# Attention core of a two-layer trunk: values as the stationary operand, probabilities scaled before they are turned

## The reference, cut to what matters

```python
# sparse heads: 8 heads in 2 groups (g) of 4 (r), head width 64, keys and values shared in a group
p_c = masked_softmax(einsum('bqgrd,bngd->bgrqn', qg, k_cmp) * scale, ...)   # 15 compressed blocks
o_c = einsum('bgrqn,bngd->bqgrd', p_c, v_cmp)
o_s = softmax over the keys of the selected blocks, times their values      # branch 0
o_w = softmax over the keys of the window, times their values               # branch 1
o_a = gates[..., 0:1] * o_c + gates[..., 1:2] * o_s + gates[..., 2:3] * o_w
# forgetting heads: 8 heads with keys and values of their own               # branch 2
s_f = einsum('bqhd,bkhd->bhqk', q, kb) * scale + cq[..., None] - cum_t[:, :, None, :]
o_b = einsum('bhqk,bkhd->bqhd', masked_softmax(s_f, causal), vb)
return concatenate([o_a, o_b], axis=-1) @ w_out
```

## Time and profile before

| | |
|---|---|
| median of three runs | 1229.42 us |
| span of the profiled execution | 1227.6 us |
| TensorE busy | 1213.1 us, 99% of the span |
| VectorE busy | 977.8 us, 80% |
| ScalarE busy | 815.7 us, 66% |
| GpSimd busy | 35.5 us, 3% |
| attention core, from its first scores to the output projection | 84.7 to 128.1 us |

### The profile page before, as it was taken

One profiled execution on the slowest core, in us unless ns is written; L12 is line 12 of the kernel. 1 busy time (PEld: TensorE's weight loads), 2 busy tenths in 40 slices (PEclk: granted clock), 3 DMA queues, 4 the chain that ended last, 5 costly groups with the idle time before them and its releaser, 6 DMA issues.

```text
span 1227.6 us, 16109 instructions
## 1 busy us (share of the span) xinstructions
PE 1213.1 (99%) x5992; PEld 1009.8 (82%) x5992; DVE 977.8 (80%) x959; ACT 815.7 (66%) x877; POOL 35.5 (3%) x41
## 2 busy tenths in 40 slices
PE   8999999999999999999999999999999999999997
PEld 6878888888898888888888888888888888888886
DVE  6998564554557478999989989889889889889896
ACT  7765354344375467777777777777777777777773
POOL 0000000000000001100000000000000000000300
PEclk9999999999999999999999999999999999999999
DMA  9730254455534256999999999999999999999992
GB/s 352 306 137 2 102 192 170 170 188 206 206 138 141 101 192 236 392 397 369 413 367 370 407 370 375 408 365 373 407 368 376 399 372 374 392 364 376 399 421 85
DMA packets 53000, 361.42 MB, mean 294 GB/s; under 512 B 6048, under 2 KB 6560, under 8 KB 10944
## 3 DMA queue, kind: packets, MB, share of 16 engines
q1 hardware_dynamic: 49872, 349.41, 73.8%
q0 software_dynamic: 3056, 11.02, 2.3%
HBM read 354.63 MB, written 5.77 MB: 294 GB/s over the span
## 4 chain that ended last, share of the span: by engine, by line
PE 96%; DVE 1%; ACT 1%; DMA 1%; SPq 0%; issue 0%; DVEq 0%
PE bank L562 29%; PE bank L564 29%; PE bank L563 29%; PE bank L1105 2%; PE bank L796 1%; PE bank L952 1%; PE bank L765 1%; DMA raw<-in_weights 1%; PE bank L572 1%; PE bank L1070 0%; PE bank L778 0%; PE bank L840 0%; ACT hT_hi L1212 0%; PE bank L1062 0%; PE bank L973 0%
## 5 line engine op out<-in xcount | busy, mean ns | idle before, releaser
L2174 DVE TENSOR_TENSOR low<-raw,whi 128x2048 fp32r<-128x2048 f32 x260 | 594.9, 2291 | 66.3 <-ACT whi L1508 59.0
L1508 ACT CAST whi<-raw 128x2048 fp32r<-128x2048 f32 x260 | 497.2, 1912 | 112.3 <-PE bank L564 111.6
L562 PE MATMUL bank<-whi,hT_hi 128*128 128x512 f32 (+1 forms) x1104 | 430.6, 390 | 0.8 <-DVE low L1660 0.5
L564 PE MATMUL bank<-whi,hT_lo 128*128 128x512 f32 (+1 forms) x1104 | 428.7, 388 | 0.0
L563 PE MATMUL bank<-low,hT_hi 128*128 128x512 f32 (+1 forms) x1104 | 428.0, 388 | 0.0
L562 PEld LDWEIGHTS bank<-whi,hT_hi 128*128 128x128 f32 x1104 | 207.4, 188 | 43.4 <-DVE hT_lo L1595 0.9
L564 PEld LDWEIGHTS bank<-whi,hT_lo 128*128 128x128 f32 x1104 | 207.3, 188 | 42.7
L563 PEld LDWEIGHTS bank<-low,hT_hi 128*128 128x128 f32 x1104 | 207.4, 188 | 41.7
L1577 DVE TENSOR_TENSOR low<-raw,whi 128x2048 fp32r<-128x2048 f32 x67 | 152.9, 2288 | 45.0 <-ACT whi L1197 44.9
L562 PE MATMUL bank<-whi,h_hi 128*128 128x512 f32 x440 | 181.0, 411 | 0.0
L564 PE MATMUL bank<-whi,h_lo 128*128 128x512 f32 x440 | 172.5, 392 | 0.0
(11 more groups left out here) (318 smaller groups left out, 779.4 us busy)
## 6 DMA issues: line engine op xcount, KB each, us to landing
raw<-in_weights SPq DMA_DIRECT2D x327, 1024.0 KB, 5.7
sums<-ybuf POOLq DMA_DIRECT2D x7, 512.0 KB, 6.8
arena<-in_compress SPq DMA_DIRECT2D x1, 1088.0 KB, 15.8
x<-in_x SPq DMA_DIRECT2D x2, 512.0 KB, 5.4
raw<-in_weights SPq DMA_DIRECT2D x4, 256.0 KB, 6.1
raw<-in_weights SPq DMA_DIRECT2D x2, 512.0 KB, 8.0
tokens<-hng POOLq DMA_DIRECT2D x2, 512.0 KB, 8.6
out<-x SPq DMA_DIRECT2D x4, 256.0 KB, 2.7
```

What stands on the lines that cost most here:

```text
L562: mm(out_, a_hi, b_hi, start=start, stop=False)
L564: return mm(out_, a_lo, b_hi, start=False, stop=stop)
L1508: nc.scalar.copy(whi[:, u % SPLIT, :, :], raw[:, u % RAW, :, :]).then_inc(S["w_hi"], 1)
L2174: V.tensor_tensor(low[:, u % RAW, :, :], raw[:, u % RAW, :, :], whi[:, u % SPLIT, :, :].bitcast(F32), ALU.subtract).then_inc(S["w_lo"], 1)
```

## The change

The value products change their operands: the 64 columns of values of a group or head are stationary, and the turned probabilities move, up to 512 columns at once. The output then has the width of a head on its partitions and positions along its columns, which is the layout that the output projection reads. The two groups of a pair (in the forgetting branch: even and odd heads) write partitions 0 to 63 and 64 to 127 of one bank.

A row of the output can no longer be scaled behind the product, since positions now lie along columns. So the probabilities are scaled before they are turned: VectorE takes the reciprocal of each unit's sums as soon as ScalarE has them, and GpSimd multiplies the unit's probabilities in place by this and by the gate of the branch, one instruction a head. `pbuf` gets four buffers. The compressed branch is scaled on VectorE, and opens the sum in bank 4 + t, to which both sparse branches are added in PSUM. The order of units is changed so that all sparse work of row tile 0 comes first, then that of row tile 1, then the forgetting heads. Work goes by pairs of units: turn both, scores of the pair after the next, value products of the pair. The scores of pairs 0 and 1 are both made ahead of the first turning. ScalarE and VectorE split the finished heads straight from banks 4 and 5; the turning of `hn` is gone. The value products of the last pair lie behind the first four blocks of the output projection. Queries get the factor minus the scale when they are copied, so that the row minimum of the scores is the bias of the exponentials without a further multiplication. The rows of the output weights are put in the new order of heads on the host.

```diff
-        pbuf = arena[:, scr0:scr0 + 1024].rearrange("p (b n) -> p b n", b=2)
+        pbuf = arena[:, scr0:scr0 + 2048].rearrange("p (b n) -> p b n", b=4)
...
+        att_pairs = [(br, 0, 0, 4) for br in range(2)] + [(br, 1, h0, 2) for br in range(2) for h0 in (0, 2)]
+        att_pairs += [(2, 0, 0, 4), (2, 1, 0, 2), (2, 1, 2, 2)]
+        att_units = [(br, t, h0 + 4 * g, n) for br, t, h0, n in att_pairs for g in range(NG)]
+        summed = {(0, 0): 2, (1, 0): 6, (0, 1): 7, (1, 1): 9}
...                                                              (GpSimd)
+            for u in range(AU):
+                br, t, h0, n = att_units[u]
+                kw = (t + 1) * P
+                pool.wait_ge(S["fac"], u + 1)
+                for h in range(h0, h0 + n):
+                    p_ = pbuf[:, u % 4, (h - h0) * kw:(h - h0 + 1) * kw]
+                    last = nc.gpsimd.tensor_scalar(p_, p_, fac[:, seq_of(u), h:h + 1],
+                                                   gates[:, t, h, br + 1:br + 2] if br < 2 else 1.0, ALU.mult, ALU.mult)
+                last.then_inc(S["scaled"], 1)
...                                                              (TensorE)
             def turn(u):
-                pe.wait_ge(S["probs"], u + 1)
+                pe.wait_ge(S["scaled"], u + 1)
...
+            def blocks_out(t):
+                for r in range(4):
+                    c = slice(r * P, (r + 1) * P)
+                    mm(bank[4 + t][:, c], vbd[:, c], pcT[:, t, :], start=(r == 0), stop=False)
+            def pv(p):
+                br, t, h0, n = att_pairs[p]
+                out_ = bank[4 + t]
+                pe.wait_ge(S["probsT"], 2 * p + 2)
+                if br == 2 and h0 == 0:
+                    pe.wait_ge(S["hT"], turned_at(1, t, 0))
+                for kt_ in range(t + 1):
+                    if br < 2:
+                        for g in range(NG):
+                            v = proj[1][:, kt_, br * P + g * HD:br * P + (g + 1) * HD]
+                            last = mm(out_[g * HD:(g + 1) * HD, h0 * P:(h0 + n) * P], v,
+                                      ptb[:, g, kt_ * n * P:(kt_ + 1) * n * P], start=False,
+                                      stop=(br == 1 and h0 + n == 4 and kt_ == t))
+                        continue
+                    for g, j in product(range(NG), range(n)):
+                        h, m = h0 + 4 * g + j, kt_ * n + j
+                        half, c = h % 2 * HD, slice(h // 2 * P, (h // 2 + 1) * P)
+                        last = mm(out_[half:half + HD, c], proj[5][:, kt_, h * HD:(h + 1) * HD],
+                                  ptb[:, g, m * P:(m + 1) * P], start=(kt_ == 0 and h < 2),
+                                  stop=(kt_ == t and h >= 6))
+                last.then_inc(S["pv"], 1)
             qk_pair(0)
             pe.wait_ge(S["cmp_pT"], 1)
             for t in range(NT):
-                mm(bank[4 + t][:, :], pcT[:, t, :], vbd, start=True, stop=True).then_inc(S["cmp_o"], 1)
-            for u in range(AU):
-                if u % 2 == 0 and u + 2 < AU:
-                    qk_pair(u + 2)
-                turn(u)
-                if u == AU - 2:
-                    transposes(hn, 1, 0, lambda half: pe.wait_ge(S["o_done"], 7))
-                if u >= 1:
-                    pv(u - 1)
-            pv(AU - 1)
-            by_tile(U_A_OUT, 0, A_OUT_BANKS[0], 1, (0, 4),
-                    lambda: transposes(hn, 1, 1, lambda half: pe.wait_ge(S["o_done"], 8)))
+                blocks_out(t)
+            qk_pair(1)
+            for p in range(AP):
+                turn(2 * p)
+                turn(2 * p + 1)
+                if p + 2 < AP:
+                    qk_pair(p + 2)
+                if p + 1 < AP:
+                    pv(p)
+            by_tile(U_A_OUT, 0, A_OUT_BANKS[0], 1, (0, 4), lambda: pv(AP - 1))
...                                                              (ScalarE)
+            for p in range(AP):
+                exponentials(2 * p)
+                exponentials(2 * p + 1)
+                if p == 3:
+                    heads_out(0, 0)
+                if p == 7:
+                    heads_out(1, 0)
+            heads_out(0, 1)
+            heads_out(1, 1)
...                                                              (VectorE)
-            V.tensor_tensor(s16, s16, bc(cm01, 2, NH), ALU.mult).then_inc(S["cmp_p"], 1)
+            V.tensor_tensor(s16, s16, bc(cm01, 2, NH), ALU.mult)
             link(V.reciprocal(sumc, sumc))
...
+            V.tensor_tensor(s16, s16, bc(f3, 3, 16), ALU.mult).then_inc(S["cmp_p"], 1)
             split(14)
...
+            for u in range(4):
+                row_least(u)
+            inverse_sums(0)
+            inverse_sums(1)
+            for p in range(AP):
+                for u in (2 * p, 2 * p + 1):
+                    probs_turned(u)
+                    if p + 1 < AP:
+                        inverse_sums(u + 2)
+                if p + 2 < AP:
+                    row_least(2 * p + 4)
+                    row_least(2 * p + 5)
+                if p == 3:
+                    heads_lower(0, 0)
+                if p == 6:
+                    heads_lower(1, 0)
+            heads_lower(0, 1)
+            heads_lower(1, 1)
```

More of the change, by code:

```diff
@@ L128, in constants @@
         seen = (ends[None, :] <= (t * P + i)[:, None])
-        c[:, C_CBIAS + 16 * t:C_CBIAS + 16 * t + NCMP] = np.where(seen, 0.0, NEG)
+        c[:, C_CBIAS + 16 * t:C_CBIAS + 16 * t + NCMP] = np.where(seen, 0.0, -NEG)
         c[:, C_CMASK + 16 * t:C_CMASK + 16 * t + NCMP] = seen
@@ L144, in masks @@
     m = np.zeros((P, 512 + P), np.float32)
-    late = np.where(i[:, None] >= i[None, :], 0.0, NEG)
+    late = np.where(i[:, None] >= i[None, :], 0.0, -NEG)
     for h in range(4):
@@ L252, in trunk @@
         fac = c0(6 * 8).rearrange("p (s h) -> p s h", s=6)
-        oacc = hn
         cg_ = Carve()
@@ L776, in turn @@
                     pe.wait_ge(S["foxT_late"], u + 1)
-                for j in range(4):
-                    last = nc.tensor.transpose(bank[2 + u % 2][:, j * P:(j + 1) * P],
-                                               pbuf[:, u % 2, j * P:(j + 1) * P], ident)
-                last.then_inc(S["probsT_psum"], 1)
[L782 to L797, removed]
+                for kt_ in range(t + 1):
+                    for j in range(n):
+                        m, c = kt_ * n + j, j * (t + 1) + kt_
+                        last = nc.tensor.transpose(bank[2 + u % 2][:, m * P:(m + 1) * P],
+                                                   pbuf[:, u % 4, c * P:(c + 1) * P], ident)
@@ L1319, in _, with exponentials @@
                     A(fz[:, 3, :], fz[:, 2, :], ACT.Ln, bias=1.0).then_inc(S["fox_l"], 1)
-            for u in range(AU):
+            def exponentials(u):
                 br, t, h0, n = att_units[u]
@@ L1847, in _ @@
-            rowmax(0)
-            rowmax(1)
-            for t in range(NT):
-                dve.wait_ge(S["cmp_o"], t + 1)
-                V.tensor_tensor(heads(oacc[:, t, 0:512]), heads(bank[4 + t][:, :]), bc(facc[:, t * 8:t * 8 + 8], 2, HD),
-                                ALU.mult).then_inc(S["o_done"], 1)
-            for u in range(AU):
-                if u + 2 < AU:
-                    rowmax(u + 2)
+                V.tensor_reduce(negm[:, seq_of(u), h0:h0 + n], score_bank(u)[:, :].rearrange("p (h n) -> p h n", h=n),
+                                AX.X, ALU.min).then_inc(S["rowmax"], 1)
@@ L1862, in _, with heads_lower @@
-            turned(1, 0)
-            take(2 * 3 - 1)
-            turned(1, 1)
+            def heads_lower(t, half):
+                at = (slice(None), slice(half * 4, half * 4 + 4), slice(t * P, (t + 1) * P))
+                dve.wait_ge(S["hT_hi"], turned_at(1, t, half * 4))
+                V.tensor_tensor(hT_lo[at], bank[4 + t][:, :].rearrange("p (k n) -> p k n", k=4),
+                                hT_hi[at].bitcast(F32), ALU.subtract).then_inc(S["hT"], 1)
+            for u in range(4):
+                row_least(u)
@@ L2261, in consumed, with heads_paired @@
     return np.array([o[0] for o in order]), np.array([o[1] for o in order])
+def heads_paired(w):
+    sparse = w[:NH * HD].reshape(NG, 4, HD, -1).transpose(1, 0, 2, 3).reshape(NH * HD, -1)
+    return np.concatenate([sparse, w[NH * HD:]])
 def layout(inp):
```

117 lines of the change are left out of this document (54 added, 63 removed).

## The result

The changed kernel takes 1232.78 us (median of 12 runs, 1230.09 to 1240.02); the kernel before, run beside it, 1231.37 (12 runs, 1229.21 to 1234.19). The ratio is 1.0028 [1.0014, 1.0041]: slower by 1.4 us in the medians and by 3.2 in the means, which five runs of 1236 us and more pull up. 1226.2 was forecast, 3.2 less than before. Its profiled execution took 1230.8 us of span, 3.2 more than before's.

What follows compares the result with a forecast made beforehand. TensorE, 99% busy, was taken as the bound: core 33.5 us of work plus waits, 40.2 against 43.6, gains 3.4; less 0.2 for the last value products, 1229.4 - 3.2 = 1226.2 us, 8-in-10 range 1223.2 to 1232.5.

Steps and rivals of the forecast that it cites:

- The clock: Rival, core: clock falls after 3 us of idle TensorE, bounded at 28 us if all the core ran so; chance 0.04.
- scaling, 128 columns: GpSimd's scaling of probabilities, first row tile: 0.34 us an instruction at 1.2 ns a column, 1.4 a unit.
- scaling, 256 columns: GpSimd's scaling of probabilities, second row tile: 0.50 us an instruction at 1.2 ns a column, 1.0 a unit.
- first, behind long rest: Start of the core: GpSimd's first scaling after a long rest is slower, 0.3 us added once.
- second wait: Start of the core: TensorE waits for the second unit's scaling, 1.4 us less 0.44 covered, so 1.0.
- a round: Steady core, per pair of units: TensorE's 3.4 us sets the pace, VectorE at some 3.1, GpSimd at 2.0.
- unit 13: Steady core: the only unit there whose transposes wait for its scaling, 0.2 us.
- wait of pair 7: End of the core: pair 7's value products wait for VectorE's queue, 1.55 us.
- hooked value products: Last pair's value products, behind the projection's first four blocks: 1.07 instead of 0.87 us, 0.2 lost.
- GpSimd as the bound: Rival, the core's 18 scalings: GpSimd sets the pace, slower than before; 1241 at 4.2 ns a column; chance 0.11.
- nothing left: Rival, core: scaling at 2.4 ns a column or dearer tile-form switches eat the gain; 3.5 lost, 1229.5 us; chance 0.16.
- column tiles in series: Rival, value products: the two column tiles run one after the other, costing 7.2 us; 1232; chance 0.06.

Runs made afterwards that it cites:

- e2: Changed kernel with 14 and 5 filler products in TensorE's two waits at the start of the core; 1228.83 us, ratio 0.9980.
- e10: e2 plus three filler products instead of one ahead of each of three groups of router logits; 1228.33 us, ratio 0.9974.
- e8: Kernel before with three filler products instead of one ahead of each of three groups of router logits; 1231.14 us, ratio 1.0003.
- e5: Kernel before with idle time alone: its first turning also waits for six GpSimd memsets; 1240.02 us, ratio 1.0075.
- e3: Changed kernel with the reciprocals of units 0 and 1 ahead of the row minima of units 2 and 3 on VectorE; 1232.15 us, ratio 1.0014.
- e6: e4 with 4 and 5 filler products in the two waits at the start of the core; 1226.00 us, ratio 0.9962.
- e4: e3 plus VectorE's low part of row tile 1's heads ahead of the row minima of units 16 and 17; 1230.34 us, ratio 0.9983.
- e7: e6 with three filler products instead of one ahead of each of three groups of router logits; 1226.08 us, ratio 0.9964.
- e11: e6 with two filler products instead of one ahead of each of three groups of router logits; 1225.15 us, ratio 0.9951.

## Why the prediction was wrong

**The step that failed** is the clock. The prediction read "The granted clock is 1.00 (2.4 GHz) throughout" off the kernel before, summed every TensorE step at it, and with the same sum put 3.1 us of idle TensorE into the core. "*The clock* falls after 3 us of idle TensorE" stood among the rivals with a chance of 0.04 and only a bound. That rival is what happened. In the core it cost 1.5 us: four transposes, eight score instructions and the mask take 1.12 + 2.00 + 0.42 = 3.54 from 95.30 on, where e2 has 0.65 + 1.06 + 0.32 = 2.03. The router stage cost 4.1 in the profiled execution, and there no rival looked at all. The sum closes: 1229.4 for the kernel before at full clock, less 2.8 for the change (e10 against e8), plus 1.5 and 4.1, is 1232.2, against 1232.57 for the profiled run, whose end behind VectorE's last addition is 0.6 longer, and 1232.78 for the median.

The Trainium skill's TensorE: Matmul & The Clock Gate (Why this matters for your kernels) warns of pauses of TensorE between bursts of matmuls, because the clock then goes back to half rate. By that rule the traces agree for the long waits: 0.50 behind 3.60 us in the changed kernel, and in e5. It does not cover e3, which fell behind 1.01 and 1.29 us, nor the router stage, where TensorE had no pause. The prediction did not weigh it.

The other steps, in its order:

| step | forecast | measured |
|---|---|---|
| compressed branch begins | 0.5 late, 86.9 | 86.80 |
| its duration | 1.84 | 2.05 |
| scores of pair 1 end | 90.4 | 90.3 |
| scaling of unit 0 begins | 91.8 | 91.79 |
| scaling, 128 columns | 0.34 | 0.43 sparse, 0.35 forgetting |
| scaling, 256 columns | 0.50 | 0.54 sparse, 0.46 forgetting |
| first, behind long rest | +0.3 | none |
| first turning | 93.5 | 93.58 |
| second wait | 1.0 | 1.29 |
| value products, a pair | 1.07 | 1.01 to 1.09 |
| a round | 3.4 | 3.43 |
| unit 13 | waits 0.2 | no wait |
| wait of pair 7 | 1.55 | 1.31 |
| projection, at full clock | near 125 | 124.93 (e2); 126.60 less 1.5 |
| hooked value products | 0.2 lost | 0.35 lost |

*GpSimd as the bound*, *nothing left* and *column tiles in series* did not come. For the scaling the table has the distance from start to start. Both sorts of units pay the same slope: 0.11 us more for 128 more columns, 0.8 to 0.9 ns a column, which is the memset's slope (0.83) and not the 1.2 taken, nor the 1.5 and 2.2 worked out as estimates. What was too low is the fixed cost of an instruction: some 0.33 us in the sparse units and 0.24 in the forgetting ones, whose second factor is a constant instead of a gate for each partition. A slope too high and a fixed cost too low nearly cancel at 256 columns (0.50 against 0.54), which is luck. They don't at 128, where a unit of four costs 0.36 more than forecast, and that is why the second wait is 1.29 and not 1.0. The transposes of the steady rounds never waited for GpSimd. Value products at 1.01 to 1.09 where the serial estimate was 1.78 say that the two column tiles run side by side. The switch between tile forms is seen once: the first projection product behind the hooked value products takes 0.43 instead of 0.23; in the core a round's 3.43 holds all its switches. The Trainium skill's TensorEngine Tiling (Array Packing), Key Properties, has a drain at such a change of mode; the row agrees, with 0.2 us here, though no run tests that the drain is the cause.

One sum of the prediction is off in itself: *nothing left*, 3.5 lost, gives 1229.7 and not 1229.5; no chance hangs on it.

The ledger as a whole was right to some tenths of a microsecond: forecast gain 3.2, gain with the clock held 2.8. The six runs at full clock with fillers at the start alone (e2) took 1226.34 to 1228.41, against the forecast of 1226.2. The changed kernel never ran so in 24 runs. That the router stage falls at all is no doing of the change: the kernel before ran below full clock in 39 of 90 runs, and fillers in that stage alone (e8) brought all 11 to full clock.

**Open.** A fall of 3.3 us at half rate lowers the mean clock by 0.0013, and every run of the changed kernel lay at 0.995 or below. So its router stage seems to fall more often than before's 4 in 10. e2 and e6, which hold the clock in the core and also reach the router stage earlier than before, were at full clock in 11 of 22 runs. In e5, whose stage begins later than before's, 5 of 6 runs have the 0.992 of its profile, which has both falls. That points at the first fall and not at the moment at which the stage begins, but no run was made to separate the two. The group of 1236 to 1240 us isn't seen in a profile. A longer fall, as e5's, does not fit it: 7 us lost to a fall lower the mean clock by 7 of 1235 us or more, 0.0057, and the runs of 1238.5 to 1240 have 0.990 or 0.991 where those near 1232.6 mostly have 0.993. A late end as in e4's profile, 7 us of idle time at half clock, lowers it by 0.0028 and would fit; that is an argument and not shown. e4 kept the clock in its profile with e3's waits.

## What to carry to other kernels

When a sum of steps leaves TensorE idle at one place for more than the trace of before ever does, the steps behind it may not be priced at before's clock: price them at both levels, and look at more than one run of before, since a stage in which the clock falls only in some runs (here the router's) is missing from a good profile. Throwaway products into a free bank during such a wait cost nothing (e2) and here decided whether the change gained or lost. And where run times fall in two groups, sort them by granted clock before comparing medians: with it held, the spread of the kernel before went from 5.2 us to 1.2 (e8, same batch) and an effect of 3 us could be read. The mean clock alone does not say where the time went: in e4's profiled run most of the lack is the idle end.

## What the runs showed of the hardware

- Waits of 3.60 and 1.29 to 1.30 us with four transposes between were followed by 3.3 us at 1.2 GHz in both profiles of the changed kernel; 1.01 and 1.29 by 3.2 in e3; 1.03 and 1.30 by none in e4; 4.64 by 7.9 in e5, where the clock had fallen within the wait.
- A stage can lose the clock while TensorE is busy without a gap: the router stage of the changed kernel has TensorE busy 16.20 of 16.20 us, with 10.2 of them at half clock. With two or three fillers in place of one ahead of three groups of logits the clock held in 32 of 32 runs (e7, e8, e10, e11).
- GpSimd's multiplication of float32, from start to start: with two factors for each partition 0.43 us for 128x128 and 0.54 for 128x256; with one such factor and a constant 0.35 and 0.46.
- The mean granted clock of a run counts the idle end: in e4 VectorE's last addition ends at 1219.0, the clock is 0.50 from 1224.0 to 1231.3, and the run has 0.995.
- Two column tiles of float32 products, 128x64 weights and up to 512 moving columns: 1.01 to 1.09 us for a pair's 1024 columns.
